# Order of the Fourier weight products, of layer 1's latents and of two splits, in a two-block model on one core

## The reference

```python
for l in range(2):                                  # first block
    shift, scale, gate = split(silu(c) @ w_ada[l] + b_ada[l], 3)
    h = layernorm(x) * (1 + scale) + shift
    u_f, z_f, cq, ckv, k_r, z_a = split(h @ w_in[l])
    f   = real(fft2(u_f, over tokens and 128 channels of 8 groups))
    y_f = (f @ w_fmix[l, group]) * silu(z_f)        # Fourier branch
    q   = rmsnorm(cq, q_norm) @ w_q_b ; kv = rmsnorm(ckv, kv_norm) @ w_kv_b
    y_a = attention(q, kv, rope(k_r)) * silu(z_a)   # 8 heads
    x = layernorm(sqrt(2) * x + gate * (concat(y_f, y_a) @ w_out[l]), ln_g, ln_b)
# second block: 16 meta tokens ahead, rms norm, causal pooling branch and convolution branch,
# two sigmoid gates, w_o, then a squared-relu MLP of 8192, with residuals and rms norms
```

## Time and profile before

| | us |
|---|---|
| median of 3 runs | 2117.17 |
| lowest, highest | 2113.32, 2117.67 |
| the profiled execution | 2116.22 |
| its span, first to last instruction | 2114.4 |
| PE busy | 2033.8 (96%) |
| VectorE busy | 1378.4 (65%) |
| ScalarE busy | 935.3 (44%) |
| mean granted TensorE clock | 0.986 |

### The profile page before, as it was taken

How to read it: one execution, slowest core, us unless ns; L and a number is a source line. 1 busy time by engine, 2 the same in 40 slices (tenths; PEclk the granted TensorE clock), 3 DMA queues, 4 the chain that set the end, 5 groups by cost and what they waited for, 6 DMA issues and landing times.

```text
span 2114.4 us, 36630 instructions
## 1 busy us (share of the span) xinstructions
PE 2033.8 (96%) x14264; PEld 1849.7 (87%) x14264; DVE 1378.4 (65%) x1891; ACT 935.3 (44%) x1390; POOL 29.9 (1%) x59
## 2 busy tenths in 40 slices
PE   5999999979999999899999999999999999999998
PEld 2779898759999987899999998889889989989986
DVE  5457677785688867888997555555545545545555
ACT  3344455454535544433346335444344434433443
POOL 0000000000000000000000000000000000000000
PEclk8999999999999999899999999999999999999999
DMA  9988888864566564354445555535555555454553
GB/s 383 394 326 306 314 314 302 336 244 182 194 234 258 224 222 184 118 179 177 179 178 180 199 179 196 201 140 184 195 195 182 189 192 189 185 197 180 188 192 137
DMA packets 64403, 462.40 MB, mean 219 GB/s; under 512 B 7264, under 2 KB 7808, under 8 KB 8368
## 3 DMA queue, kind: packets, MB, share of 16 engines
q1 hardware_dynamic: 57152, 410.49, 52.7%
q0 software_dynamic: 7152, 50.51, 6.4%
HBM read 458.85 MB, written 2.13 MB: 218 GB/s over the span
## 4 chain that ended last, share of the span: by engine, by line
PE 67%; DVE 8%; ACT 2%; issue 1%; DVEq 0%; ACTq 0%
PE ps L523 22%; PE ps L525 22%; PE ps L524 22%; DVE w_lo L1695 3%; DVE area L1731 1%; ACT w_hi L1149 1%; PE ps L565 1%; DVE st L1715 1%; ACT sc L1401 0%; ACT sc L1407 0%; DVE X L2163 0%; DVE grow L2260 0%; DVE csil L2107 0%; DVE area L2260 0%; DVE rs L2022 0%
## 5 line engine op out<-in xcount | busy, mean ns | idle before, releaser
L1695 DVE TENSOR_TENSOR w_lo<-raw,w_hi 128x1024 fp32r<-128x1024 f32 x642 | 758.7, 1221 | 393.3 <-ACT w_hi L1149 390.2
L523 PE MATMUL ps<-a_hi,w_lo 128*128 128x256 f32 (+1 forms) x2912 | 830.6, 285 | 13.3 <-DVE w_lo L1695 7.3
L1149 ACT CAST w_hi<-raw 128x1024 fp32r<-128x1024 f32 (+1 forms) x642 | 640.7, 1047 | 455.6 <-PE ps L525 440.0
L524 PE MATMUL ps<-a_lo,w_hi 128*128 128x256 f32 (+1 forms) x2912 | 826.2, 284 | 0.0
L525 PE MATMUL ps<-a_hi,w_hi 128*128 128x256 f32 (+1 forms) x2912 | 824.8, 283 | 0.0
L523 PEld LDWEIGHTS ps<-a_hi,w_lo 128*128 128x128 f32 x2912 | 554.6, 190 | 42.0 <-issue 32.9
L525 PEld LDWEIGHTS ps<-a_hi,w_hi 128*128 128x128 f32 x2912 | 554.5, 190 | 0.0
L524 PEld LDWEIGHTS ps<-a_lo,w_hi 128*128 128x128 f32 x2912 | 552.0, 190 | 0.7 <-issue 0.5
L523 PE MATMUL ps<-w_hi,y_lo 128*128 128x512 f32 x720 | 281.4, 391 | 1.3 <-DVE w_lo L1695 1.3
L524 PE MATMUL ps<-w_lo,y_hi 128*128 128x512 f32 x720 | 280.3, 389 | 0.0
L525 PE MATMUL ps<-w_hi,y_hi 128*128 128x512 f32 x720 | 280.2, 389 | 0.0
(11 more groups left out here) (274 smaller groups left out, 2050.8 us busy)
## 6 DMA issues: line engine op xcount, KB each, us to landing
raw<-in_stream SPq DMA_DIRECT2D x331, 1024.0 KB, 4.8
area<-in_ada SPq DMA_DIRECT2D x46, 1024.0 KB, 8.0
area<-in_ada POOLq DMA_DIRECT2D x40, 1024.0 KB, 5.4
grow<-in_ada SPq DMA_DIRECT2D x10, 1024.0 KB, 6.1
area<-in_rows POOLq DMA_DIRECT2D x4, 1024.0 KB, 6.6
X<-in_x SPq DMA_DIRECT2D x1, 2048.0 KB, 7.7
grow<-row_scratch POOLq DMA_DIRECT2D x2, 1024.0 KB, 6.4
grow<-in_rows POOLq DMA_DIRECT2D x2, 1024.0 KB, 5.1
```

The costliest lines, as they stand in the source:

```text
L523: pe.matmul(o, w[1], a[0], start=first, stop=False, skip_group_check=shared)
L524: pe.matmul(o, w[0], a[1], start=False, stop=False, skip_group_check=shared)
L1149: ac.copy(to, raw[:, bass.ds((g % RAW) * CH + h * n, n)]).then_inc(hi_ready, 1)
L1695: ve.tensor_tensor(to, raw[:, bass.ds((g % RAW) * CH + h * n, n)], hi.bitcast(F32), ALU.subtract).then_inc(lo_ready, 1)
```

## The change

Five edits of order and one of banks.

```diff
-CW_BANKS = (2, 3, 2, 3)
+CW_BANKS = (2, 3, 0, 1)
@@ PE, fourier_weights
                     if j < 2:
                         half(g, j)
+                    elif j == 2:
+                        pe.wait_ge(uk_l, l + 1)
                     else:
-                        pe.wait_ge(cw_l, 4 * l + j - 1)
+                        pe.wait_ge(z_ready, 16 * l + 2)
@@ PE, last_quarter
-                pieces(l, 3, 1, range(2))
+                pieces(l, 3, 1)
...
-                fourier_weights(l, (0, 1))
-                pieces(l, 3, 1, range(2, 4))
-                fourier_weights(l, (2, 3))
+                fourier_weights(l, range(4))
                 pieces(l, 3, 2)
@@ ACT
                 gate_tanh(bank(1, T))
+                early(12)
                 cw(0)
                 cw(1)
-                early(12)
...
-                group(4)
...
-                latents(range(3))
+                if l:
+                    latents(range(3))
+                group(4)
+                latents(range(3 * l, 3 + 3 * l))
                 group(5)
-                latents(range(3, QT + CT))
+                if l == 0:
+                    latents(range(3, QT + CT))
@@ DVE
                 gate(1, bank(1, T), kept_z)
+                early(12)
                 cw(0)
                 cw(1)
                 ada_early(2)
-                early(12)
...
+                def lat_rstd():
+
+                    ve.wait_ge(ln_std, NORM[f"lat{l}"] + 1)
+                    own.link(ve.reciprocal(rs[:, :], rs[:, :]))
+
                 ada_early(4)
+                if l:
+                    lat_rstd()
                 early(L_DFT + 3)
...
-                    if tiles_[0] == 0:
-                        ve.wait_ge(ln_std, NORM[f"lat{l}"] + 1)
-                        own.link(ve.reciprocal(rs[:, :], rs[:, :]))
+                    if l == 0 and tiles_[0] == 0:
+                        lat_rstd()
...
+                if l:
+                    latents(range(3))
                 group(4)
-                latents(range(3))
+                latents(range(3 * l, 3 + 3 * l))
                 group(5)
-                latents(range(3, QT + CT))
+                if l == 0:
+                    latents(range(3, QT + CT))
@@ DVE, end of W_out
                 last_split(g + 12, 1, False)
+                last_split(g + 12, 2, False)
                 z_block(2, 0)
+                last_split(g + 12, 3, False)
                 z_block(2, 1)
-                last_split(g + 12, 2, False)
-                last_split(g + 12, 3, False)
```

## The result

| | before | after |
|---|---|---|
| median, same comparison | 2115.24 (2112.46 to 2117.67, 4 runs) | 2102.23 (2101.36 to 2105.26, 4 runs) |
| profiled execution, span | 2116.22, 2114.4 | 2105.26, 2103.5 |
| mean granted clock | 0.986 | 0.989 |

The ratio is 0.9944 [0.9928, 0.9959]: faster, by 11.8 us of 2115. The changed kernel was run again in two later comparisons: 2104.56 and 2103.22, ratios 0.9954 [0.9941, 0.9968] and 0.9944 [0.9927, 0.9961]. All 15 runs of it together have a median of 2103.55 (mean 2103.74, standard deviation 1.9). The 92 runs of the kernel before, from all comparisons, have a median of 2114.84 (mean 2114.58, deviation 2.8).

What follows compares the result with a forecast made beforehand. PE is busy 96% of the span, so only its waits can be won. Gains 2.8 + 0.5 + 4.8 + 0.6 + 0.5 = 9.2 us take 2116.22 to 2107.0, median 2107.9, stated as 2107.8; range 2104 to 2113.2.

Steps and rivals of the forecast that it cites:

- Last quarter, layer 1: End of layer 1's first projections: both PE stops go, 0.1 lost at seq_dft(0); gain 2.8 us, bounds 0.7 to 3.1.
- Last quarter, layer 0: Same stops in layer 0, mostly handed back as three small waits behind an adaLN step; gain 0.5 us, bounds -0.4 to 2.9.
- Latents: Layer 1, groups 5 and 6: reciprocal and latents moved earlier; 3.3 us of stops plus 1.5 of clock, 4.8, bounds 1.2 to 5.4.
- group 6 has no latents ahead of it any more: Layer 1's group 6 keeps PE's pace as group 7 does; no gain was put on it.
- Splits: End of each layer's W_out: split ahead of two z_blocks removes PE's stop; gain 0.6 us in layer 1, 0.5 in layer 0.
- The 0.2 taken off for the row's DMA: Layer 0's end: the earlier raw load runs beside lnb's row transfer, landing it 0 to 1.2 us later; 0.2 deducted.
- the base of the sum: Whole kernel: profiled execution of 2116.22 us and a median of three runs 0.95 above it, from which 9.2 was taken.
- The range's lower end: Whole kernel: 2104 us, if the stop at 1403 loses its 1.5 dip and latents and layer ends reach upper bounds.
- Rival A: VectorE's chain decides both last quarters and the clock's dip returns elsewhere; gain 5.7 us, 2111.5; chance 0.2.
- B: Layer 1's latents only move the stop and the clock falls again; latents 1.0 us, total 5.4, 2111.8; chance 0.1.
- D: Work behind 145 us shifts against the clock's window, seven more dips cost 10.5 us against 9.2; slower, 2118.5; chance 0.04.
- Rival C: Layer 0 is paced by its DMAs and keeps nothing of its 1.0 us; the rest stays, 8.2, 2109; chance 0.1.

Runs made afterwards that it cites:

- e7_late12: Kernel before with four product banks and PE's new last-quarter order, but the last block's split still behind cw(0) and cw(1); 2115.7 us, ratio 1.0009.
- e8_tuned: Changed kernel with layer 0's adaLN step behind early(L_Z2), t_part(0) ahead of the third latent square, row-sum matmul behind group 3's u chunk; 2104.07 us, 0.9952.
- e9_tuned2: As e8_tuned, but the row sums' matmul stands between the two halves of group 3's u chunk; 2099.77 us, ratio 0.9932.
- e11_before: The kernel before, unchanged, compared with itself and profiled a second time; 2115.47 us, ratio 0.9999.
- e2_latents: Kernel before with only layer 1's reciprocal moved behind ACT's root and latents 0 to 2 ahead of group 4; 2111.0 us, ratio 0.9976.
- e5_recip: Kernel before with only layer 1's reciprocal moved up behind ACT's root, latents left in place; 2110.34 us, ratio 0.9983.
- e12_move: Repeat of e6_move against the kernel before, for a second profile and more runs; 2111.92 us, ratio 0.9988.
- e3_splits: Kernel before with only the two splits of W_out's last blocks moved ahead of the z_blocks; 2115.69 us, ratio 0.9999.
- e6_move: Kernel before with layer 1's reciprocal and latents 0 to 2 together ahead of group 4; 2113.61 us, ratio 0.9999.
- e1_quarter: Kernel before with only the last quarter's edits: four products in one run in four banks, last block's split ahead of cw; 2109.89 us, ratio 0.998.

## Why the prediction was right in its steps and too small in its sum

- **Last quarter, layer 1: right.** 2.9 for 2.8. The margin ahead of the last block held, with 0.1 of its 0.18: ACT's split starts at 547.42, 2.37 later is 549.79, and PE starts at 549.91. And seq_dft(0) had no stop above the 0.1 of the forecast that shows. e7_late12 shows that the gain hangs on the split's place, as was argued.
- **Last quarter, layer 0: right in kind, low by 0.2.** Three waits where three were named, 0.77, 0.18 and 1.04 (the first with its 0.16), for 0.6, 0.4 and 1.2 of the forecast. e8_tuned and e9_tuned2 support the cause given: with the adaLN step behind early(L_Z2), and t_part(0) moved with it, the stage has the full 3.1. No run moves the adaLN step alone.
- **Latents: right in size, wrong in one cause.** 3.4 and 1.5 for 3.3 and 1.5; the wait left is 0.42 (0.58 lost) for 0.6. But of the 1.5 that was put to the clock only 0.84 is clock. The other 0.65 belongs to the step "group 6 has no latents ahead of it any more", which was costed at nothing, and it could not be seen before: at the lower clock PE was late enough for t_lo.
- **Splits: right for layer 1 (0.7 for 0.6); layer 0's 0.7 for 0.5 is in part luck.** The 0.2 taken off for the row's DMA didn't come, nor did the 0.2 that the row sum was to hold back: PE's stop went whole, and 0.28 was lost to a stop that the forecast doesn't have.
- **The step that failed: the base of the sum ("I say 2107.8", from a median of three runs), and the width put around it.** The forecast went from 2116.22 and the median of three to 2107.8. Against the 2114.84 of 92 runs the same 9.2 gives 2105.6, and the 9.9 measured in stages gives 2104.9, for 2103.55 of 15 runs (2102.23 of the first four). The difference of the means, 10.8 with about 1.1 to each side, holds the 9.9 and just reaches the 9.7. The sum failed by 0.7 (0.2 at each of layer 0's two steps, 0.1 at each of the others), the level by 2.2, and the first four runs lay 1.3 below what 15 give. What is left, 1.4 by the medians and 0.9 by the means, the stages don't hold. A part of it may be the clock: the 15 timed runs have a mean of 0.9889 for the 0.9870 of before, and layer 1's dip accounts for 0.0008 of that. The other 0.0011 would be 1.2 us by the estimate of the last section; whether the new order or chance brings it is not shown.
- **The range's lower end**, 2104.0, was made of one dip and the upper bounds of two terms, and took the base for certain, though its three runs spread over 4.4 us. It allowed for the dip behind 1403 only. The trace of before has a longer one right ahead of it, which the forecast didn't read: the clock was 0.50 over 1384 to 1390.
```profile
1384.00:1390.00 6.00, 4.73 (x23) 4.36 (x22) 4.09 (x10) 2.74 (x8) 0.00 (x0) 0.50 0.38 153
```
The two, 2.2 and 1.5 us, came together in seven of the 14 profiles and neither came in the other seven, so 3.7 us hung on one draw.

- **Rival A** (VectorE decides, the clock's dip comes back): no. Layer 1 kept 2.9, and no lower level followed groups 5 and 6 in any profile without their stops. **B** (the latents move the stop): no, 0.42 was left. **D** (slower by the clock): no; 3.2 to 12.5 us of matmul time per execution are lost to the lower level in the profiles of all kernels, and the changed one has 4.6, 5.1 and 7.6 for the 12.0 and 10.3 of before.
- **Rival C** (layer 0 is DMA-paced): open in part. The profile after has a stop that before lacks. PE's row of the changed kernel in layer 0's W_out, then VectorE's that came before it:
```profile
436.21 0.50 PE L523 MATMUL ps<-w_hi,y_lo 128*128 128x512 f32 x1 [3.24 <-DVE w_lo L1697]
...
430.49 2.35 DVE L1733 SCALAR_TENSOR_TENSOR area<-area,csil 128x2048 f32<-128x2048 f32 x1 [3.43 <-DMA area<-in_ada]
```
VectorE sits in its queue before a chunk of w_ada that has not landed, and the split behind it is late. The same in e11_before, whose code is the kernel before:
```profile
433.52 0.50 PE L523 MATMUL ps<-w_hi,y_lo 128*128 128x512 f32 x1 [1.40 <-DVE w_lo L1695]
...
427.80 2.35 DVE L1731 SCALAR_TENSOR_TENSOR area<-area,csil 128x2048 f32<-128x2048 f32 x1 [2.73 <-DMA area<-in_ada]
```
The stop is in 11 of the 14 profiles. Where layer 0 has no edit up to there, it is 1.40 in e11_before, 1.53 in e2_latents, 1.80 in e5_recip and 0.67 in e12_move, and under 0.1 in before, e3_splits and e6_move. So it comes without the change. All seven with an edited last quarter have it: 3.24, 1.50 and 1.90 in the changed kernel's three, 2.30 in e1_quarter, 2.12 in e7_late12, 1.02 in e8_tuned, 2.17 in e9_tuned2. The means are 2.0 and 0.8, so the edit may make it longer and hand back what layer 0 won. Against that, it doesn't follow PE's lead: by its stages e7_late12 comes to it 2 us late and has 2.12, e8_tuned 2 us early and has 1.02. No run removes the adaLN chunk's wait alone, so this stays open.

The stop also covers the last row of the table of stages. In e1_quarter, e5_recip and e7_late12, which don't have the edit of the splits, the stop of 0.89 at the end of W_out is gone too, since PE comes late to it (PE has no wait from 438 to 462 in e5_recip). In e11_before and e2_latents, with shorter stops at 433, it is still there with 1.12 and 1.24. So in an execution with a stop of 1.8 us or more, such as the profiled one, layer 0's 0.7 is not the edit's.

**Where the profiled pair got its 11.** Its spans differ by 10.9: 9.9 of stages, 6.4 of less lower clock in unchanged places (1.6 at the start of layer 1, 1.1 at the start of the second block, 2.2 at the MLP's start, 1.5 behind the stop at 1403), and against them 4.7 of stop and lower clock at 436, with 0.7 of small differences. (The 9.9 counts layer 0's end, and the 4.7 takes it off again.) A reader who takes the difference of two single executions for the effect adds the three up to the right size by accident.

## What to carry to other kernels

Price a step of an in-order queue by following the queue to the next item that someone waits for, and count what leaves the queue too, since what looks harmless beside a lower clock may be a wait of its own. A long operation with an early input (here a reciprocal of 3.34 us) belongs in the first real gap, and the split that feeds the next matmuls belongs ahead of the copies and z_blocks that only clear banks. Take the level of a kernel from many runs and the effect of an edit from stages that repeat within 0.1 us, and put the scatter of the level on both sides of the range.

## What the runs showed of the hardware

The lower clock level after a short stop of PE came and went at the same stops. The pair of stops of 1.7 and 1.9 us around groups 5 and 6 was followed by it in before, e1_quarter, e3_splits and e11_before (1.4 to 1.5 us of matmul time lost each time) and not in e7_late12. The stop at 1403, 1.87 or 1.88 us long, is in all 14 profiles. In e11_before and then in e9_tuned2, the window from 0.5 ahead of its end:
```profile
1402.00:1408.00 6.00, 5.51 (x33) 5.51 (x34) 4.71 (x6) 5.97 (x7) 0.00 (x0) 0.72 0.48 173
```
```profile
1387.00:1393.00 6.00, 5.55 (x46) 5.55 (x47) 4.71 (x6) 5.97 (x7) 0.00 (x0) 1.00 0.50 175
```
The same busy times stand there, once at 0.72 and once at 1.00, and 33 matmuls got through in the one and 46 in the other. It was followed by the lower level in 7 of 14 profiles, 1.5 us each time. These are the seven in which the level was also low behind the stop at 1383.

The loss is counted as the distance of PE's starts less the distance that the same matmuls have at 1.00. Behind the first 60 us it is 12.0 us in before, 10.3 in e11_before, 4.6, 5.1 and 7.6 in the changed kernel's profiles and 3.2 in e9_tuned2. 3.2 of it is in every profile: the 15 transposes behind each of the two longest pauses (9.8 and 8.9 us) start 0.213 apart, where later ones start 0.109 apart.

The clocks listed with the timed runs show that this spread goes with the time. Of 88 runs of the kernel before, the 18 with a mean clock of 0.985 took 2116.4 us in the mean and the 19 with 0.989 took 2112.0, so 0.001 of mean clock goes with 1.1 us. Within one clock value the runs still spread by 1.6 to 1.9 (standard deviation), which the clock, given to 0.001, doesn't explain.
